# Long convolution with its tokens sorted by parity: inverse on half of the frequencies, second filter made beside the first product

## The reference, cut to what matters

```python
def hyena_filters(L, w1, b1, w2, b2, w3, freq):
    ...
    h = jnp.sin(freq[0] * (z @ w1.astype(f32) + b1.astype(f32)))
    h = jnp.sin(freq[1] * (h @ w2.astype(f32) + b2.astype(f32)))
    h = (h @ w3.astype(f32)).reshape(L, HYENA_ORDER, 2, HYENA_WIDTH)
    ...
    return h * decay[:, None, None, :]

def bidir_kernel(hf, hb):
    zero = jnp.zeros((1, hf.shape[1]), hf.dtype)
    return jnp.concatenate([hf, zero, hb[:0:-1]], axis=0)

def fftconv(u, k, bias):
    L = u.shape[1]
    U = jnp.fft.rfft(u, n=2 * L, axis=1)
    K = jnp.fft.rfft(k, axis=0)
    y = jnp.fft.irfft(U * K[None], n=2 * L, axis=1)[:, :L]
    return y + u * bias.astype(jnp.float32)

# in first_block
        z = v.astype(f32)
        for n, gate in enumerate((x1, x2)):
            k = bidir_kernel(filt[:, n, 0], filt[:, n, 1])
            z = gate.astype(f32) * fftconv(z, k, filt_bias[l, n])
        y_b = z.astype(dt) @ w_b_out[l]
```

## Time and profile before

| | |
|---|---|
| median of 3 runs | 2789.38 us (2789.16 to 2790.26) |
| the profiled execution | 2789.46 us |
| its span in the trace | 2787.5 us |
| PE busy | 2387.6 us, 86% |
| PE weight loads busy | 1863.7 us, 67% |
| DVE busy | 1166.8 us, 42% |
| ACT busy | 840.8 us, 30% |
| mean granted clock of PE | 0.912 |
| DMA | 669.80 MB, 240 GB/s |

### The profile page before, as it was taken

One profiled execution on the slowest core, in us unless ns is written; L12 is line 12 of the kernel. 1 busy time (PEld: TensorE's weight loads), 2 busy tenths in 40 slices (PEclk: granted clock), 3 DMA queues, 4 the chain that ended last, 5 costly groups with the idle time before them and its releaser, 6 DMA issues.

```text
span 2787.5 us, 43857 instructions
## 1 busy us (share of the span) xinstructions
PE 2387.6 (86%) x18628; PEld 1863.7 (67%) x18628; DVE 1166.8 (42%) x1678; ACT 840.8 (30%) x1198; POOL 111.8 (4%) x107
## 2 busy tenths in 40 slices
PE   6899989767777777767679997889999999688999
PEld 6896486323233333222269995789999999488999
DVE  6757552000000000000045567566556556755655
ACT  3384121100000000000034444344445444434543
POOL 0000012000000000000010001000001000200000
PEclk9999998887878988887889997899999999699999
DMA  6435047999999999999965541143555554022553
GB/s 226 147 126 175 16 182 300 425 425 426 425 424 425 425 424 426 425 425 426 425 261 182 182 161 59 36 149 122 183 183 202 182 182 159 1 93 98 177 184 117
DMA packets 118618, 669.80 MB, mean 240 GB/s; under 512 B 10682, under 2 KB 12901, under 8 KB 60992
## 3 DMA queue, kind: packets, MB, share of 16 engines
q1 hardware_dynamic: 113376, 650.14, 59.8%
q0 software_dynamic: 2784, 13.21, 1.4%
q10 hardware_dynamic: 2304, 4.20, 0.4%
HBM read 662.26 MB, written 5.24 MB: 239 GB/s over the span
## 4 chain that ended last, share of the span: by engine, by line
PE 54%; DMA 20%; DVE 8%; SPq 7%; issue 3%; ACT 3%; DVEq 3%; POOLq 1%; POOL 0%; ACTq 0%; PEldq 0%; PEld 0%
PE psd L566 29%; PE psx L566 8%; DMA ring<-in_w_up 8%; SPq L2454 7%; DMA e_w_lo<-in_w_gate 3%; DMA hx<-in_w_down 3%; PE psd L835 3%; DVE w_lo L1662 2%; DMA ring<-in_w_down 2%; DMA ring<-in_w_gate 2%; DVE scr L1662 1%; PE psd L826 1%; PE psd L863 1%; PE psx L1072 1%; PE psx L739 1%
## 5 line engine op out<-in xcount | busy, mean ns | idle before, releaser
L566 PE MATMUL psd<-h_hi,w_hi 128*128 128x256 f32 x2448 | 703.0, 287 | 34.9 <-DVE h_lo L1662 12.8
L1662 DVE TENSOR_TENSOR w_lo<-ring,w_hi 128x1024 fp32r<-128x1024 f32 x436 | 524.0, 1242 | 436.3 <-ACT w_hi L1276 433.8
L566 PE MATMUL psd<-h_lo,w_hi 128*128 128x256 f32 x2448 | 696.8, 285 | 0.0
L566 PE MATMUL psd<-h_hi,w_lo 128*128 128x256 f32 x2448 | 696.5, 285 | 0.0
L1276 ACT ACTIVATE w_hi<-ring 128x1024 fp32r<-128x1024 f32 x436 | 435.2, 1046 | 304.7 <-PE psd L566 299.4
L566 PEld LDWEIGHTS psd<-h_hi,w_hi 128*128 128x128 f32 x2448 | 474.0, 194 | 40.8 <-issue 30.8
L566 PEld LDWEIGHTS psd<-h_lo,w_hi 128*128 128x128 f32 x2448 | 474.2, 194 | 0.3
L566 PEld LDWEIGHTS psd<-h_hi,w_lo 128*128 128x128 f32 x2448 | 474.0, 194 | 0.0
L566 PE MATMUL psx<-halves,w_hi 128*128 128x256 f32 x1408 | 255.6, 283 | 3.2 <-issue 3.2
L1662 DVE TENSOR_TENSOR scr<-psd,scr 128x512 f32<-128x512 f32 x20 | 13.8, 690 | 498.0 <-PE psd L835 498.0
L566 PEld LDWEIGHTS psx<-halves,w_hi 128*128 128x128 f32 x1408 | 219.6, 192 | 3.9 <-issue 3.9
(11 more groups left out here) (354 smaller groups left out, 2786.0 us busy)
## 6 DMA issues: line engine op xcount, KB each, us to landing
ring<-in_ffn_wi SPq DMA_DIRECT2D x88, 1024.0 KB, 4.8
scr<-in_w_gate SPq DMA_DIRECT2D x48, 1024.0 KB, 19.7
scr<-in_w_down SPq DMA_DIRECT2D x48, 1024.0 KB, 22.4
scr<-in_w_up SPq DMA_DIRECT2D x48, 1024.0 KB, 27.0
ring<-in_ffn_wo SPq DMA_DIRECT2D x44, 1024.0 KB, 4.9
ring<-in_w_gate SPq DMA_DIRECT2D x32, 1024.0 KB, 19.1
ring<-in_w_up SPq DMA_DIRECT2D x32, 1024.0 KB, 26.7
ring<-in_w_down SPq DMA_DIRECT2D x32, 1024.0 KB, 22.9
```

What stands on the lines that cost most here:

```text
L566: mm = pe.matmul(o, w[u], a[v], start=start and i == 0, stop=stop and i == 2, **kw)
L1662: return dve.tensor_tensor(o, a, b, op)
```

## The change

**What it does.**

- Tokens are sorted by parity. The transposes that bring the signal to token rows, and the taps' products, take every second token (`tt::TT`), so that `tt` is now the parity. The angle of the second 128 frequencies is then that of the first, mirrored: `fwd` holds a sign in place of a second set, and the inverse of each parity needs 128 sums or 128 differences only.
- After the product of spectra, DVE adds and subtracts the two halves of the frequencies into `folds` (two instructions of 1024 columns per half of the channels). The inverses take those: 2 products of 512 columns per bank for 4, and for the second filter 8 of 128 columns for 8 of 256. `z` is put back in the order of tokens by DVE's last write.
- The second filter's taps are made right behind the first's, and PE's order mixes taps and spectra (`filter_order`). Its spectra come behind the first signal's forward products and before the first inverses. Its taps lie in the buffers of `w_hi` and `w_lo` that slot w_b_out 1 uses, so that slot is cut later: `prime` instead of `cut_ahead` at w_a_out 3.
- The filter's second layer is made twice, on rows 0 to 63 and 64 to 127, and the two directions of the taps are taken from one or the other (`r`).
- The result is cut piece by piece, and `dense` of w_b_out 0 waits piece by piece. The loads of `memT` and of the experts' first slots wait for the last piece.

**The diff**, cut to its core:

```diff
...
+
+    th = np.pi * (2 * np.arange(P, dtype=np.float64) + 1) / (2 * T)
+    t = 2 * np.arange(P)[:, None] + np.arange(2)[None, :]
+    cos, sin = np.cos(t[:, :, None] * th), np.sin(t[:, :, None] * th)
+    sign = np.array([1.0, -1.0])[None, :, None]
+    fwd = np.stack([cos, sign * cos, -sin, -sign * sin], axis=2)
+    inv = np.stack([cos, -sin], axis=2).transpose(3, 1, 2, 0) / T
+    dft = np.concatenate([fwd.reshape(P, 4 * T), inv.reshape(P, 2 * T)], axis=1)
...
             plan += [(((part, l), i), reader) for i in range(count)]
         ffn(l, "ffn2")
     return plan
+
+
+def filter_order():
+
+    taps = [("taps", n, half, tt, d) for n in range(2) for half in range(2) for tt in range(TT) for d in range(2)]
+    spec = [("spec_k", 0, half, m) for half in range(2) for m in range(4)]
+    return (taps[0:6] + spec[0:1] + taps[6:7] + spec[1:2] + taps[7:8] + spec[2:3] + taps[8:10] + spec[3:4] + taps[10:12]
...
+        w3h, bias_row = [at(56, 2, 512), at(8, 2, 512)], [at(60, D, parts=1), at(12, D, parts=1)]
+        decay, spec_k, spec_y = at(64, TT, D), at(72, 4, D), at(16, 4, 512)
+        waiting = dense_at[SN[("w_b_out", 1)]] % 2
+        taps_of = [[hx_at(8 * half, 2, TT, 512) for half in range(2)],
+                   [e[:, :].rearrange("p (i a c) -> p i a c", i=2, a=TT) for e in ((e_hi0, e_lo0), (e_hi1, e_lo1))[waiting]]]
+        folds = [[hx_at(8 * half, TT, 2, 512) for half in range(2)], [at(64, TT, 2, 512), at(40, TT, 2, 512)]]
+        taps_f = [sq[:, 4:8, :].rearrange("p (d a) t -> p d (a t)", d=2), at(20, 2, 512)]
+        fwd, inv = at(0, TT, 2 * T), at(4, TT, 2, P)
...
-                                          sq[:, 2 * (i % 2) + m, tt * P:(tt + 1) * P], ident)
+                                          sq[:, 2 * (i % 2) + m, tt::TT], ident)
...
+            def taps(n, half, tt, d):
+
+                if (half, tt, d) == (0, 0, 0):
+                    pe.wait_ge(S(f"w3_in{n}"), 32)
+                r = slice(64 * d, 64 * d + 64)
+                b = XB.claim(pe, ("taps", n, half, tt, d))
+                done(pe.matmul(b[:, :], sq[r, 2, tt::TT], w3h[n][r, half, :], start=True, stop=True))
+
+            def spectrum(n, half, m):
+
+                if m == 0:
+                    pe.wait_ge(S("taps_ready"), 2 * n + half + 1)
+                b = XB.claim(pe, ("spec_k", n, half, m))
+                for tt in range(TT):
+                    mm = pe.matmul(b[:, :], fwd[:, tt, m * P:(m + 1) * P], taps_of[n][half][:, m // 2, tt, :],
+                                   start=(tt == 0), stop=(tt == 1))
+                done(mm)
+
+            for kind, *at_ in filter_order():
+                if kind == "taps":
+                    taps(*at_)
+                else:
+                    spectrum(*at_)
...
+                if n == 0:
+                    for half in range(2):
+                        for m in range(4):
+                            spectrum(1, half, m)
                 for i in range(4):
-                    if i % 2 == 0:
-                        pe.wait_ge(S("spec_y"), 4 * n + i + 2)
+                    half, j = divmod(i, 2)
+                    if j == 0:
+                        pe.wait_ge(S("spec_y"), 2 * n + half + 1)
+                    y = folds[n][half]
                     b = XB.claim(pe, ("inv", n, i))
                     if n == 0:
-                        tt, half = i % 2, i // 2
-                        for m in range(4):
-                            mm = pe.matmul(b[:, :], inv[:, m, tt * P:(tt + 1) * P],
-                                           spec_y[:, m, half * 512:(half + 1) * 512], start=(m == 0), stop=(m == 3))
+                        for c in range(2):
+                            mm = pe.matmul(b[:, :], inv[:, j, c, :], y[:, j, c, :], start=(c == 0), stop=(c == 1))
                     else:
-                        for c in range(2):
-                            for m in range(4):
-                                mm = pe.matmul(m2(b)[:, c, :], spec_y[:, m, (2 * i + c) * P:(2 * i + c + 1) * P],
-                                               inv[:, m, :], start=(m == 0), stop=(m == 3))
+                        for ch in range(2):
+                            col = (2 * j + ch) * P
+                            for tt in range(TT):
+                                for c in range(2):
+                                    mm = pe.matmul(m2(b)[:, ch, tt * P:(tt + 1) * P], y[:, tt, c, col:col + P],
+                                                   inv[:, tt, c, :], start=(c == 0), stop=(c == 1))
                     done(mm)
-            pe.wait_ge(S("z_cut"), 1)
             for i in range(4):
...
                 cut_ahead(cutter, ("w_a_out", 2 * i))
                 act.wait_ge(S("filt_red"), i + 1)
-                act.activation(sq[0:64, 1 + i, :], sq[0:64, 1 + i, :], ACT.Sin).then_inc(S("filt_sin"), 1)
-            cut_ahead(cutter, ("w_a_out", 3))
...
+                act.activation(v, v, ACT.Sin).then_inc(S("filt_sin"), 1)
+            prime(cutter, ("w_a_out", 3))
             for tt in (0, 1):
...
             act.drain().then_inc(S("decay"), 1)
             for n in range(2):
                 for half in range(2):
+                    if n:
...
 
             def gate_a(i):
-                cut_ahead(cutter, ("w_a_out", i))
+                (cut_ahead if i < 3 else prime)(cutter, ("w_a_out", i))
...
-                        tt_(taps_s[:, tt, cs], f0, f1, ALU.add)
-                        tt_(taps_d[:, tt, cs], f0, f1, ALU.subtract)
-                        dve.drain()
+                        for im, op in enumerate((ALU.add, ALU.subtract)):
+                            ins = tt_(taps_of[n][half][:, im, tt, :], f[:, 0, :], f[:, 1, :], op)
                     dve.drain().then_inc(S("taps_ready"), 1)
+            for n in range(2):
...
-                        dve.drain().then_inc(S("spec_y"), 1)
+                        dve.drain()
+                    for tt, op in enumerate((ALU.add, ALU.subtract)):
+                        ins = tt_(folds[n][half][:, tt, :, :], spec_y[:, 0:3:2, :], spec_y[:, 1:4:2, :], op)
+                    dve.drain().then_inc(S("spec_y"), 1)
...
                     else:
-                        read(tt_(x2[:, 2 * i:2 * i + 2, :], m2(b), x2[:, 2 * i:2 * i + 2, :], ALU.mult))
-                    if n == 0 and i % 2:
-                        dve.drain().then_inc(S("z_tok"), 2)
-            cut_acts(x2, "z_cut")
+                        z = x2[:, 2 * i:2 * i + 2, :].rearrange("p c (n t) -> p c t n", t=TT)
+                        read(tt_(z, m2(b).rearrange("p c (t n) -> p c t n", t=TT), z, ALU.mult))
+                        dve.drain().then_inc(S("act_made"), 1)
+                        if i:
+                            low(x2, h_hi, h_lo, i - 1, "z_cut")
+            low(x2, h_hi, h_lo, 3, "z_cut")
...
-            load(filt_w[0:64, 64:128], A["filt_w2"], "filt_in")
+            for c in (64, 128):
+                load(filt_w[0:64, c:c + 64], A["filt_w2"], "filt_in")
...
+
+            w3 = A["filt_w3"].rearrange("i (n d h c) -> n d i h c", n=2, d=2, h=2)
+
+            for n in range(2):
+                for d in range(2):
+                    load(w3h[n][64 * d:64 * d + 64, :, :], w3[n, d], f"w3_in{n}")
+                load(bias_row[n], A["filt_bias"][:, n * D:(n + 1) * D], f"bias_in{n}")
...
+            pool.wait_ge(S("z_cut"), 4)
             load(mem[:, :, :], A["memT"].rearrange("(k p) t -> p k t", p=P), "mem_in")
...
                 if s == ERING_SCR:
-                    sp.wait_ge(S("z_cut"), 1)
+                    sp.wait_ge(S("z_cut"), 4)
```

More of the change, by code:

```diff
@@ L233, in small_plan @@
     add("dve", "filt", 1)
+    for kind, *at in filter_order():
+        add("dve" if kind == "taps" else "act", kind, *at)
     for n in range(2):
-        for half in range(2):
-            for tt in range(TT):
-                for d in range(2):
-                    add("dve", "taps", n, half, tt, d)
-        for half in range(2):
-            for m in range(4):
-                add("act", "spec_k", n, half, m)
         for half in range(2):
@@ L245, in small_plan @@
                     add("dve", "spec_u", n, half, f, im)
+        if n == 0:
+            for half in range(2):
+                for m in range(4):
+                    add("act", "spec_k", 1, half, m)
         for i in range(4):
@@ L719, in _ @@
             b = XB.claim(pe, ("filt", 1))
-            done(pe.matmul(b[0:64, 0:T], filt_w[0:64, 64:128], sq[0:64, 1, :], start=True, stop=True))
+            done(pe.matmul(b[:, 0:T], filt_w[0:64, 64:192], sq[0:64, 1, :], start=True, stop=True))
             dense(("w_a_out", 3))
@@ L1425, in _ @@
                 for half in range(2):
+                    if n:
+                        act.wait_ge(S("spec_y"), half + 1)
                     for m in range(4):
@@ L1900, in _ @@
             dve.wait_ge(S("decay"), 1)
-            bias_row = at(8, 2, D, parts=1)
```

(4 more changed lines are left out.)

65 lines of the change are left out of this document (21 added, 44 removed).

## The result

| | before | after |
|---|---|---|
| median | 2789.82 us (4 runs, 2789.16 to 2792.34) | 2766.26 us (4 runs, 2763.55 to 2770.12) |
| ratio, 95% interval | | 0.9917 (0.9903 to 0.9930) |
| the profiled execution | 2789.46 us | 2770.12 us |
| its span | 2787.5 us | 2768.3 us |
| PE busy | 2387.6 us | 2372.6 us |

With the five runs of a repeat the changed kernel has nine runs, from 2763.55 to 2770.12, median 2767.7, and the kernel before stands at 2789.7 to 2790.1 in the groups of runs further on: 22 us. Some 6 to 8 us more were gained than forecast. Taken over nine runs the time stands at the very edge of the range (2767.7 for 2767.5).

What follows compares the result with a forecast made beforehand. TensorE, busy 86% of the span, was taken as the bound, the experts' start hanging on its chain. Three stretches put w_b_out's first product at 352.5 instead of 368.15: 2789.5 - 15.7 = 2773.8 us, range 2767.5 to 2781.

Steps and rivals of the forecast that it cites:

- First stretch: Convolution, all taps and first spectra: PE ends last, at 290.0, after DVE's first half of taps at 264.8.
- All three corrections: Taps and first spectra: paired 64-row products save 1.7 us, twelve 64/128-row changes cost 1.5, half clock loses 3.0.
- Second stretch: Convolution, forward products, second spectra, first inverses: 27.5 plus 6.9 plus 1.0 of waiting, together 35.4 us, to 325.4.
- Third stretch: Convolution, second product: DVE is the longer, folds add 5.0 us, last inverses 3.6; ends at 352.5.
- Behind it: From the last inverse into w_b_out: pieces taken as cut, so the 4.05 us gap goes; w_b_out 1's cut stays hidden.
- the new wait: PE's 5.5 us idle before the last two inverses, let cost the same 1.8 us of clock as the old gap.
- The clock hardly falls: Rival: no clock loss at the taps, free tiling changes, last inverses at full clock; 22.0 us gained, 2767.5; chance 0.15.
- Clock back at 280: Rival, taps and first spectra: 15.2 us at half speed, 7.6 lost instead of 3.0; 2778.4; chance 0.12.
- the slower case: Rival: half clock through spectra into forward products; gain gone if until about 302, up to 39 us slower, 2828; chance 0.02.
- the swallowed gain: Rival: before the experts, a load or cut that did not move takes the gain; 2789; chance 0.05.
- unhalved inverses: Rival, second inverses: 128-column products take as long as 256-column ones; 3.4 us on the path, 2777.2; chance 0.02.
- The terms set at nothing: Queues: POOL's four more loads, memT's later load (5 us if not) and w_o 1's load were each to cost nothing.

Runs made afterwards that it cites:

- before_warm: Kernel before, with four fp32 products of 512 columns filling PE's idle 4.05 us ahead of w_b_out; 2787.4 us, ratio 0.999.
- after_whole: Changed kernel with the result cut in one go behind the last inverse and w_b_out waiting for all of it; median 6.8 us above the nine runs' 2767.7.
- after_seq: Changed kernel without the mixed order: first filter's taps, then its spectra, then the second filter's taps; 2774.8 us.
- after_warm_inv: Changed kernel with five fp32 products of 512 columns filling PE's idle 5.09 us ahead of the last two banks of inverses; 2768.8 us.
- after_again: Changed kernel run once more, unaltered; 2768.3 us (2764.95 to 2769.86).
- before_again: Kernel before run once more, unaltered; 2789.0 us, ratio 0.9996.
- before_pieces: Kernel before, with w_b_out 0 taking the pieces of the convolution's result as they are cut; 2786.1 us, ratio 0.9986.

## Why the prediction was wrong

**First stretch** (35.5 us forecast, 33.8 measured). DVE's first taps came 3.7 us after PE's (3.6 forecast), the first spectra 10.3 (10.3). All three corrections were mis-sized. In the timeline above a single taps product and a pair of opposite halves both take 1.06 us from start to next start (274.80 to 275.86, 277.77 to 278.83): the second product costs nothing, four pairs save 3.4 us, not 1.7. I had leaned on the earlier trace rows, in which narrow products hide only in part. The Trainium skill (TensorE: Matmul & The Clock Gate, Why this matters for your kernels) says of small-K products in distinct row groups that they run concurrently; the trace agrees: the first four taps products, all on rows 0 to 63, took 3.70 us before, and now, two on each half of the rows, 2.00. A change costs 1.06 - 0.86 = 0.20, and again 280.75 - 278.83 - 4 x 0.43 = 0.20: 2.4 for twelve, my upper bound, not 1.5. The clock was back 14.6 us after the taps' start (forecast 16.3), and cost less: from 267.81 to 271.53 it is 3.72 us where 1.92 is the rule, and then 1.35 for 1.06, so 2.1 were lost, not 3.0. In all 22.4 - 3.4 + 2.4 + 2.1 = 23.5, as the window has it.

**Second stretch**: 35.4 forecast, 326.75 - 291.32 = 35.4.

**Third stretch**: 27.1 forecast, 28.8 measured. The folds take 2.36 for two, the halved inverses 3.81 for two banks (3.6), and the first result follows the last fold as forecast. The excess is the last inverses at half clock, 5.78. I had this loss, as 1.8, in the step behind it ("no difference"); that it stands here is why 15.7 came out, and that is luck: -1.7 in the first stretch against +1.7 here.

**Behind it** the step that failed is "I take every microsecond by which w_b_out's first product moves as a microsecond of the total". Three things were gained beyond it:
- w_b_out 0 runs at full clock, 5.76 for 7.54: 1.8 us. I had set it off against the new wait, but the new wait's price was already paid in the 98.0.
- Behind w_o's wait of 3.01 us the clock does not fall in either trace of the changed kernel: the rest of `dense`, 2.2 us in the first pair of traces and 1.3 in the second, where w_b_out 0 had lost more. That wait is not touched by the change, and has the same length in both.
- The half clock in the router is shorter: 3.1 us in the first pair of traces, 0.1 in the second. This part is not firm.

Together 3.8 to 7.1; with 15.7 in the convolution (17.2 in the second pair, where the kernel before lost another 1.5 to the clock), less 0.6 for the transposes, about 20 to 22 us. The medians say 22 to 24; the rest is within what the first 250 us and the second block scatter. The first belongs to the release of w_b_out: before_warm and after_whole show it from both sides. Of the second the runs show only that it goes with edits ahead of it. after_whole brings the clock's fall back, but so do after_seq and after_warm_inv, which keep the release; so two rivals are not excluded: that any shift of what stands ahead of w_o's wait can do it, and that single executions differ. The cause of this part stays open.

Two of the prediction's own signs of being wrong came: a clock below 1.00 after 280 (0.73 and 0.63 around the last inverses, in the windows above), and the experts earlier by more than w_b_out is.

**The rivals.** "The clock hardly falls" (2767.5) came nearest in time, but not by its mechanism: the clock fell at the taps and at the last inverses. Clock back at 280, the slower case, the swallowed gain and unhalved inverses are all refuted by the rows above. The terms set at nothing (POOL's loads, `memT`, w_o 1) show no new wait of PE.

## What to carry to other kernels

A wait costs its length and the half clock behind it, and an edit that brings, takes or shifts a wait can go together with a change of clock at a later wait, itself unchanged: undoing one release of 4.1 us was worth 6.8. Filling such waits with products raised the clock at the place and made no kernel clearly faster; in after_warm_inv the clock fell further on instead. So a shift in a kernel with many short waits is not carried rigidly; give the range a clock term of a few microseconds for each wait behind the change, on the side of gain as well. Before a repeat or an undoing, a trace alone can't tell which of these differences belong to the change.

## What was unexpected of the hardware

The same wait, w_o's 3.01 us, at the same place in the program, once with the clock falling behind it and once without. PE's timeline in the kernel before, and then in after_again; the same two passes take 0.80 us and 0.51:

```profile
400.27 0.80 PE L566 MATMUL psd<-halves,w_hi 128*128 128x256 f32 x2 [3.02 <-DVE halves L1662]
```

```profile
384.13 0.51 PE L578 MATMUL psd<-halves,w_hi 128*128 128x256 f32 x2 [3.01 <-DVE halves L1689]
```

Eleven traces have this wait at 3.01 us, and the clock fell behind it in six: before, before_again, before_warm, after_whole, after_warm_inv, after_seq. In the two that have it at 2.07 it did not. The Trainium skill (TensorE: Matmul & The Clock Gate, Why this matters for your kernels) advises against idle gaps above a certain length; here one length went both ways, and behind the shorter early waits of 2.35 and 2.02 us the clock fell in nine traces of fourteen. Length alone does not decide, nor does the gap ahead of w_b_out: before_pieces has one, of 2.31 us, and no fall at w_o; after_seq and after_warm_inv have none and the fall. Nor does the time from the span's start: at w_o, waits that began at 381.12 (after_again) and 381.40 (after_warm_inv) went different ways, and so did early ones that began at 169.04 (before_pieces) and 169.10 (before). The early ones sort by when the first dense product started, some 145 us before. What decides stays open; it differs between executions of programs that are all but equal up to there, and no run here varied it alone.

DVE's addition of two 128x512 tiles took 1.58 us beside POOL's multiplication and 0.69 without it. The Trainium skill (SBUF — State Buffer, SBUF: two separate sides) has a DVE instruction with two inputs in SBUF and a POOL instruction that reads SBUF wait for one another at a port that they share; the trace agrees: the 0.89 us more are most of the 1.03 that POOL's instruction of that moment took.
